# Inverting the delta rule's triangular matrix by diagonal blocks of 32 instead of in full 128 x 128 matrices

## The chip, the cores and the metric

One core of one Trainium2 chip runs the whole program. The metric is the device time of one execution in microseconds (us); the kernel before has a median of 3261.0 us over three runs (3259.91 to 3263.16).

## What is computed

One layer of a hybrid decoder for 2048 prompt tokens and 8 x 4 sample tokens: RMSNorm, one input projection (1024 to 3608 columns), a gated linear attention (GLA) group and a gated delta rule (GDN) group of four heads each, an output projection, then a gated MLP with a convolution, and a last RMSNorm. Everything is in float32. The change touches one step of the delta rule, which the reference has as a triangular solve in each chunk:

```python
kk = jnp.einsum('bhid,bhjd->bhij', ki, ki)
L = jnp.where(strict, bi[..., :, None] * kk * decay, 0.0)
eG = jnp.exp(G)[..., None]
rhs = bi[..., None] * (vi - eG * jnp.einsum('bhid,bhdv->bhiv', ki, h))
U = lax.linalg.triangular_solve(L + eye, rhs, left_side=True, lower=True, unit_diagonal=True)
```

## The kernel before, in words

The program has two halves. `mixers` runs everything up to the output projection and the second norm, `mlp` the rest. The change lies in `mixers` alone.

`mixers` walks over 16 tiles of 128 tokens (`t` from 0 to 15, `C` = 128) and then over one tile of the 32 sample tokens (`S` = 32). Each engine has its own hand-written list of instructions, in order, and they meet by semaphores. TensorE's list is the spine: its function `mixer` interleaves the mixer of tile t with large matmuls of other tiles. These come through `fill(i, j)`, which issues parts i to j-1 of 40: an even part under 16 is two steps of the output projection of tile t-1 (`project_out`, L744), any other part is two steps of the input projection of tile t+2 (`project`, L710; for the last prompt tile `project_sample`, L728, which has nothing from part 24 on). One part of `project` is 2 matmuls of 128x128 weights by 451 columns, which the profile shows as 4 MATMUL instructions: each float32 matmul is two of them.

The matrix of the delta rule is made and inverted like this, for four heads at once, each a 128 x 128 matrix with the heads side by side (512 columns):

- TensorE makes k k^T in bank 5 (L907) and q k^T in bank 7 (L911); VectorE multiplies the first by the decay (`lt`, L1671) and sets `s_lt_made`; then come the squares' sum (L1675), `ab` (L1678), `kh` (L1683), three small ones (L1688 to L1691), `vb` (L1693) and the scaled q (L1697).
- The inverse is built by doubling, level by level: `a` = 0 to 6 joins diagonal blocks of span 1, 2, 4, ... 64 (`SPANS`, `l` = 6 - `a`). GpSimd cuts out the part of `lt` that belongs to the level with a mask of 0 and 1 (`ltm`, L647, 128 x 512) and clears the other half of a product buffer (`pp`, L654).
- In level `a` TensorE computes `P` = L_a^T times the inverse `xi` (in `block_products`, L940 for the whole width and L945 for strips of 32 or 64 columns), VectorE scales it by -beta (L1754), and TensorE makes both the update of the inverse and that of its transpose `xit`, so two products into banks 3 and 4. VectorE adds them to `xi` (L1785) and `xit` (L1789). Level 0 takes transposes in place of products (L972, L1008). In level 5 only `xi` is updated; in level 6 `xi` is turned (L978), VectorE copies a part of it (L1777), and only `xit` is updated.
- `xit` and `vb` give U (L1022), U the state update (L1049) and the output (L1055, L1056). Only `xit` is read after the inverse.

Between these steps TensorE's list holds fills: part 22 after L972, 23 after `P` of level 1, then one or two parts after each product group, up to part 36 before L1022. `turn_y(0)` and `turn_y(1)` (L770) turn the normed output of tile t-1 in level 1; `turn_y(1)` waits until ScalarE has emptied the bank of projection group 3, whose last part is fill 23 (L1170). `turn_mixed(0)` (L934) stands before level 5. VectorE does other things in the same levels: `keep_gla` (L1703) in level 0, `sum_squares` (L1727) and `keep_y_half` (L1470, twice) in level 1, `subtract_known` (L1713) in level 2, `gate_out(0)` (L1735) in level 3. SyncE's list issues the DMAs in a fixed order.

The instruction of the level products, where `k` is a strip of 32 or 64 rows of the result, so that four or two strips stand in different column groups of the array:

```python
width = max(S, 2 * SPANS[l])
for b in range(0, N, width):
    k = slice(b, b + width)
    x = pe.matmul(packed(out[k, b // 2:(b + width) // 2], l), left[:, k], blocks(right[:, k], l, r),
                  start=True, stop=True)
```

## Time and profile before

| | |
|---|---|
| device time, three runs | 3259.91, 3261.0, 3263.16 us |
| span of the profiled execution, first to last instruction | 3255.5 us |
| median of the runs less this span | 5.5 us |
| TensorE busy over the span | 3173.5 us (97%) |
| VectorE, ScalarE, GpSimd busy | 2029.6, 833.7, 580.7 us |
| mean granted TensorE clock | 0.988 of full speed |
| `mixers` (until the MLP's first matmul) | 1600.66 us |

No time of its own is given for the profiled execution, so the 5.5 us around its span is taken from the runs' median. Engines: PE is TensorE's matmul, DVE VectorE, ACT ScalarE, POOL GpSimd, SPq the queue of SyncE, which issues DMAs. A row of the timeline gives start, length, engine, line, operation, tensors, shapes, and the count of instructions merged in it; lengths of merged matmuls overlap the next row's start, since matmuls are pipelined, so what a group costs is read from its start to the start of the next group. For TensorE a shape such as 128*32 128x16 is the weights' rows times their columns, then the rows and columns of what is streamed.

### The profile page before, as it was taken

To read this page: it belongs to the slowest core of one execution; us is meant where nothing else is said; L and a number is where in the kernel's file an instruction comes from. 1 tells how busy PE (TensorE), PEld (TensorE's weight loads), DVE (VectorE), ACT (ScalarE), POOL (GpSimd) and SP (SyncE) were. 2 spreads that over 40 slices of the span, in tenths; PEclk is the share of its full clock that TensorE was granted. 3 is DMA by queue.
4 is the path that set the end of the run, shared out by engine and by line. 5 is a ranking of instruction groups with operands and counts; after the bars stand their busy time and mean duration, and the time that the engine had idled before them with its cause. 6 is when DMAs were issued, how large, how long until landed. Compare 5 with 4: busy or idle time off the path is not lost.

```text
span 3255.5 us, 56610 instructions
## 1 busy us (share of the span) xinstructions
PE 3173.5 (97%) x22353; PEld 2088.1 (64%) x22353; DVE 2029.6 (62%) x4672; ACT 833.7 (26%) x1743; POOL 580.7 (18%) x935
## 2 busy tenths in 40 slices
PE   7999999999999999997799999999999999999998
PEld 4555565566655565554577777777767767777765
DVE  2556666655566665655565666666676666666668
ACT  2222333223223333233321112111232211221213
POOL 1111111111111110112331211121053121111110
PEclk9999999999999999997899999999999999999999
DMA  7022222222222222215611111111133111111112
GB/s 242 27 67 85 85 77 75 85 67 69 66 75 85 85 66 85 80 52 159 205 50 39 52 52 39 39 52 39 39 124 119 48 43 52 39 39 39 47 31 78
DMA packets 223188, 236.37 MB, mean 73 GB/s; under 512 B 14204, under 2 KB 167332, under 8 KB 222931
## 3 DMA queue, kind: packets, MB, share of 16 engines
q1 hardware_dynamic: 222931, 232.81, 22.7%
q8 instruction: 177, 2.90, 0.4%
q14 instruction: 80, 0.66, 0.1%
HBM read 203.10 MB, written 29.67 MB: 72 GB/s over the span
## 4 chain that ended last, share of the span: by engine, by line
PE 50%; DVE 1%; issue 0%; ACT 0%; DVEq 0%
PE mlp_bank L2139 33%; PE mlp_bank L2213 15%; PE mlp_bank L2227 2%; PE mlp_bank L2219 0%; DVE mcv L2588 0%; DVE arena L2552 0%; DVE acc L2649 0%; DVE arena L2553 0%; PE mlp_bank L2238 0%; ACT raw L2331 0%; PE mlp_bank L2225 0%; DVE mcv L2592 0%; DVE arena L2560 0%; DVE arena L2557 0%; DVE raw L2520 0%
## 5 line engine op out<-in xcount | busy, mean ns | idle before, releaser
L710 PE MATMUL mixer_bank<-arena,hnt 128*128 128x451 f32 x2048 | 862.5, 552 | 9.2 <-DMA arena<-in_w_in_dram 8.4
L2139 PE MATMUL mlp_bank<-arena,ws 128*128 128x256 f32 (+1 forms) x2816 | 646.2, 383 | 3.8 <-DVE raw L2526 3.8
L2139 PEld LDWEIGHTS mlp_bank<-arena,ws 128*128 128x128 f32 x2816 | 535.7, 190 | 85.8 <-DVE raw L2526 4.6
L710 PEld LDWEIGHTS mixer_bank<-arena,hnt 128*128 128x128 f32 x2048 | 365.8, 190 | 298.0 <-issue 291.5
L2213 PE MATMUL mlp_bank<-arena 128*128 128x512 f32 x1120 | 493.8, 593 | 1.0 <-DVE arena L2560 1.0
L2621 DVE TENSOR_TENSOR acc<-acc,mlp_bank 128x512 f32<-128x512 f32 x560 | 370.8, 686 | 55.5 <-PE mlp_bank L2213 54.8
L2213 PEld LDWEIGHTS mlp_bank<-arena 128*128 128x128 f32 x1120 | 213.1, 190 | 235.2 <-issue 206.2
L647 POOL TENSOR_TENSOR ex<-dtt,level 128x512 f32<-128x512 f32 (+1 forms) x114 | 142.9, 1254 | 935.6 <-DVE dtt L1671 637.3
L2588 DVE SCALAR_TENSOR_TENSOR mcv<-raw,cf,mcv 128x512 f32<-128x512 f32 (+2 forms) x352 | 262.8, 762 | 50.3 <-ACT mcv L2302 41.5
L2139 PE MATMUL mlp_bank<-arena 128*128 128x256 f32 (+1 forms) x1056 | 250.1, 387 | 5.6 <-PEq L2731 4.6
L744 PE MATMUL mixer_bank<-wo,th 128*128 128x512 f32 x512 | 248.0, 607 | 2.9 <-DMA wo<-in_w_out_dram 2.2
L2139 PE MATMUL mlp_bank<-arena,wu 128*128 128x256 f32 (+1 forms) x1056 | 246.1, 383 | 0.9 <-ACT raw L2331 0.9
L2139 PEld LDWEIGHTS mlp_bank<-arena 128*128 128x128 f32 x1056 | 202.1, 192 | 57.3 <-issue 26.6
L2139 PEld LDWEIGHTS mlp_bank<-arena,wu 128*128 128x128 f32 x1056 | 200.8, 190 | 48.9 <-issue 19.1
L1170 ACT ACTIVATE proj<-mixer_bank,x_rs 128x451 f32<-128x451 f32 x128 | 81.3, 635 | 558.3 <-PE mixer_bank L710 526.4
L2532 DVE TENSOR_TENSOR raw<-raw,mlp_bank 128x256 f32<-128x256 f32 (+1 forms) x88 | 37.5, 426 | 273.9 <-PE mlp_bank L2139 273.9
L2285 ACT COPY raw<-mlp_bank 128x256 f32<-128x256 f32 (+1 forms) x88 | 33.1, 376 | 494.4 <-PE mlp_bank L2139 494.4
L744 PEld LDWEIGHTS mixer_bank<-wo,th 128*128 128x128 f32 x512 | 93.4, 191 | 100.7 <-issue 89.8
L2526 DVE TENSOR_TENSOR raw<-raw,mlp_bank 128x256 f32<-128x256 f32 (+1 forms) x88 | 37.4, 425 | 190.1 <-ACT raw L2331 190.1
L1522 DVE SCALAR_TENSOR_TENSOR cv<-cx,cw,cv 128x128 f32<-128x128 f32 x576 | 154.7, 345 | 0.0
L2302 ACT ACTIVATE mcv<-raw,cf 128x512 f32<-128x512 f32 (+2 forms) x176 | 127.0, 721 | 103.4 <-DVE raw L2532 90.3
L1785 DVE TENSOR_TENSOR qe<-qe,mixer_bank 128x256 f32<-128x256 f32 x80 | 33.9, 424 | 127.0 <-PE mixer_bank L945 127.0
(368 smaller groups left out, 3577.9 us busy)
## 6 DMA issues: line engine op xcount, KB each, us to landing
wo<-in_w_out_dram SPq DMA_DIRECT2D x260, 256.0 KB, 2.9
arena<-in_w_up_dram SPq DMA_DIRECT2D x44, 512.0 KB, 4.9
wu<-in_w_up_dram SPq DMA_DIRECT2D x44, 512.0 KB, 4.9
arena<-in_w_down_dram SPq DMA_DIRECT2D x40, 512.0 KB, 4.0
arena<-in_w_in_dram SPq DMA_DIRECT2D x7, 1804.0 KB, 16.0
xc<-in_x_t_dram SPq DMA_DIRECT2D x16, 512.0 KB, 4.3
xt<-in_x_prompt_dram SPq DMA_DIRECT2D x16, 512.0 KB, 5.0
xr<-in_x_prompt_dram SPq DMA_DIRECT2D x16, 512.0 KB, 3.6
```

The costliest lines, as they stand in the source:

```text
L647: gp.tensor_tensor(ltm[0:N, :, 0:N], lt[0:N, :, 0:N], level[0:N, l, 0:N].unsqueeze(1).to_broadcast([N, H, N]), ALU.mult)\
L710: x = pe.matmul(bank[ring(g)][0:N, 0:GW], hnt[:, k, 0:N], w[:, k, g * GW:(g + 1) * GW], start=(k == 0), stop=(k == KT - 1))
L744: pe.matmul(bank[e if t == TILES else 0][0:N, :], mixt[k // H][:, k % H, 0:N], wo[i % 4][:, :], start=(k == 0), stop=(k == KT - 1)).then_i ...
L1170: act.activation(proj[0:N, g * GW:(g + 1) * GW], bank[ring(g)][0:N, 0:GW], ACT.Identity, scale=x_rs[0:N, :]).then_inc(s_proj_out, 1)
L1522: x = dve.scalar_tensor_tensor(out=dst, in0=src, scalar=cw[:, c, tap:tap + 1], in1=dst, op0=ALU.mult, op1=ALU.add)
L2139: x = pe.matmul(out[:, 0:N], left[:, k, :], xb[:, slot, k, g * N:(g + 1) * N], start=first and k == 0, stop=k == HK - 1, skip_group_check= ...
L2213: pe.matmul(bank[4 + o % 4][:, :], left, right, start=True, stop=True).then_inc(s_down_done, 1)
L2227: x = pe.matmul(out[0:N, :], act_[a + j][:, t * C:t * C + N], right[j][:, e * 512:e * 512 + 512], start=(j == 0 and t < 8), stop=(j == 1))
L2302: act.activation(cv[e][:, 0:n], raw[p][e][:, c0:c0 + n], ACT.Identity, scale=cf[p][:, e, 0:1])\
L2532: dve.tensor_tensor(v, v, q_bank[:, 0:N], ALU.add).then_inc(s_q2_added, 1)
L2588: x = dve.scalar_tensor_tensor(out=dst, in0=src, scalar=w, in1=dst, op0=ALU.mult, op1=ALU.add)
L2621: dve.tensor_tensor(v, v, bank[4 + o % 4][:, :], ALU.add).then_inc(s_y_added, 1)
```

## The change

For the prompt tiles the inverse is kept as the four diagonal blocks of 32 rows, one below the other in 128 partitions and 32 columns a head (`xd`, 128 x 128 for all heads), until span 16 is joined.

- VectorE makes the four diagonal blocks of `lt` first, in four instructions of 32 partitions by 128 columns (`ld`), and the other columns, 32 to 127, after the squares' sum. GpSimd cuts all five small levels out of `ld` at once (`lsm`, five instructions of 128 x 128), clears `xit`, and later makes the copy of the blocks' lower three quarters (`xa`) with a column of 0 and 1.
- Level 0: VectorE turns `lsm`'s first level (32 x 32 blocks), scales and adds the unit matrix in four instructions, and turns the result (`xdt`). TensorE has nothing to do in this level; the fill 22 that stood between its two steps stands ahead of level 1.
- Levels 1 to 4: TensorE's product has 32 rows by 32 columns of weights and 16 columns streamed, for four heads and four blocks, all into bank 5; the update is a single product of the same size into bank 3. VectorE scales (128 x 64), adds (128 x 64), and turns `xd` into `xdt` (128 x 128) itself; in level 4 it turns the four blocks into `xit`.
- Level 5 multiplies only the single 32 x 32 blocks (8 products, then 12), level 6 single 64 x 64 blocks (4, then 4), with plain copies by VectorE in place of additions.
- The masks `level` are half as wide; `small`, `unit_s` and `below` are new and set up once, the copies of the first two by seven VectorE instructions before tile 0. The sample tile keeps its two levels; one of its weight buffers moves from `level` to `cx`.

```diff
         uu = shared(ex_, 2)
+        xa = qe_[:, 0:256].rearrange("p (h i) -> p h i", h=H)
+        xd = xa[:, :, 0:S]
+        newd = qe_[:, 256:512]
+        lsm = qe_[:, 1024:1024 + NS * H * S].rearrange("p (a h i) -> p a h i", a=NS, h=H)
+        xdt, l0, ld = (ex_[:, 128 * i:128 * i + 128].rearrange("p (h i) -> p h i", h=H) for i in range(3))
...
@@ -205,8 +214,9 @@
         uu_s = ltm[:, 0, :]
         kh_s = kh[:, 0, :]
         wo_s = [proj[:, 512 * i:512 * i + 512] for i in range(7)]
-        wo_s += [v.rearrange("p a b -> p (a b)") for v in (level[:, 0:4, :], qka[:, :, :], lt[:, :, :],
+        wo_s += [v.rearrange("p a b -> p (a b)") for v in (qka[:, :, :], lt[:, :, :],
                                                            hgla[:, :, :], hgdn[:, :, :])]
+        wo_s.insert(7, cx[:, :, :].rearrange("p c i -> p (c i)")[:, 1048:1560])
...
-                inv = list(reversed(levels))
-                base = NL * t
-                for a, l in enumerate(inv):
-                    turned_later = not sample and a == NL - 2
+                if not sample:
+                    gp.wait_ge(s_rows_copied, 1)
+                    gp.wait_ge(s_ld_made, n)
+                    for a in range(NS):
+                        gp.tensor_tensor(lsm[:, a, :, :], ld[:, :, :],
+                                         small[:, NS - 1 - a, :].unsqueeze(1).to_broadcast([C, H, S]), ALU.mult)\
+                            .then_inc(s_ltm_made, 1)
+                    gp.memset(xit[:, :, :], 0.0).then_inc(s_x_sides, 1)
+                    gp.wait_ge(s_x_sides, 2 * t + 1)
+                    gp.wait_ge(s_xi_new, 6 * t + 5)
+                    gp.tensor_scalar(xa[:, :, S:2 * S], xd, below[:, :], None, ALU.mult).then_inc(s_x_sides, 1)
+                    return
...
-                        continue
+                        sample_gla_out(2 * a + 1)
+                    inv_done = 7 * t + 2
+                else:
+                    quads = [slice(S * b, S * b + S) for b in range(4)]
+                    fill(22, 23)
+                    for a in range(1, NS):
+                        l = NL - 1 - a
+                        if a == 1:
+                            pe.wait_ge(s_lt_made, n)
+                        pe.wait_ge(s_ltm_made, NS * t + a + 1)
+                        pe.wait_ge(s_xi_new, 6 * t + a)
+                        for h, r in every(range(H), quads):
+                            x = pe.matmul(packed(bank[5][r, 16 * h:16 * h + 16], l), lsm[r, a, h, :],
+                                          blocks(xd[r, h, :], l, 0), start=True, stop=True)
+                        x.then_inc(s_p_done, 1)
+                        if a == 1:
+                            turn_y(0)
+                        fill(22 + 2 * a - (a == 1), 23 + 2 * a - (a == 1))
+                        if a == 1:
+                            pe.wait_ge(s_kh_made, n)
+                        pe.wait_ge(s_p_out, 6 * t + a)
+                        pe.wait_ge(s_xit_new, 7 * t + a)
+                        for h, r in every(range(H), quads):
+                            x = pe.matmul(bank[3][r, 16 * h:16 * h + 16], xdt[r, h, :],
+                                          newd[r, 16 * h:16 * h + 16], start=True, stop=True)
+                        x.then_inc(s_dx_done, 1)
+                        if a == 1:
+                            turn_y(1)
+                            fill(24, 25)
+                        fill(23 + 2 * a, 24 + 2 * a)
+                    turn_mixed(0)
+                    pe.wait_ge(s_xi_new, 6 * t + 5)
+                    for h, (lo, hi) in every(range(H), ((quads[0], quads[1]), (quads[2], quads[3]))):
+                        x = pe.matmul(bank[5][hi, S * h:S * h + S], lt[lo, h, hi], xd[lo, h, :], start=True, stop=True)
+                    x.then_inc(s_p_done, 1)
+                    fill(32, 33)
+                    pe.wait_ge(s_p_out, 6 * t + 5)
+                    pe.wait_ge(s_vb_made, n)
+                    pe.wait_ge(s_xit_new, 7 * t + 5)
...
+                        pe.matmul(bank[3][quads[1], S * h:S * h + S], xit[quads[1], h, quads[1]],
+                                  newd[quads[1], S * h:S * h + S], start=True, stop=True)
+                        for lo, hi in ((quads[0], quads[1]), (quads[2], quads[3])):
+                            x = pe.matmul(bank[4][lo, S * h:S * h + S], newd[hi, S * h:S * h + S], xit[hi, h, hi],
+                                          start=True, stop=True)
                     x.then_inc(s_dx_done, 1)
...
+                    fill(33, 34)
+                    lo, hi = slice(0, 64), slice(64, 128)
+                    pe.wait_ge(s_xi_new, 6 * t + 6)
+                    for h in range(H):
+                        x = pe.matmul(bank[5][hi, 64 * h:64 * h + 64], lt[lo, h, hi], xa[lo, h, :], start=True, stop=True)
+                    x.then_inc(s_p_done, 1)
+                    fill(34, 35)
+                    pe.wait_ge(s_p_out, 6 * t + 6)
+                    pe.wait_ge(s_xit_new, 7 * t + 6)
+                    for h in range(H):
+                        x = pe.matmul(bank[4][lo, 64 * h:64 * h + 64], newd[hi, 64 * h:64 * h + 64], xit[hi, h, hi],
+                                      start=True, stop=True)
+                    x.then_inc(s_dx_done, 1)
+                    fill(35, 36)
+                    inv_done = 7 * n
...
                 dve.wait_ge(s_kk_done, n)
-                dve.wait_ge(s_ltm_made, NL * t)
-                dve.tensor_tensor(lt[0:N, :, 0:N], heads(5)[0:N, :, 0:N], dtt[0:N, :, 0:N], ALU.mult)\
-                    .then_inc(s_lt_made, 1)
+                dve.wait_ge(s_ltm_made, NS * t)
+                if sample:
+                    dve.tensor_tensor(lt[0:N, :, 0:N], heads(5)[0:N, :, 0:N], dtt[0:N, :, 0:N], ALU.mult)\
+                        .then_inc(s_lt_made, 1)
+                else:
+                    for b in range(4):
+                        r = slice(S * b, S * b + S)
+                        x = dve.tensor_tensor(ld[r, :, :], heads(5)[r, :, r], dtt[r, :, r], ALU.mult)
+                    x.then_inc(s_ld_made, 1)
                 dve.wait_ge(s_k_squared, n)
                 dve.wait_ge(s_k_lned, t)
                 dve.tensor_reduce(kss[0:N, :], ksq[0:N, :, :], AX_X, ALU.add).then_inc(s_k_summed, 1)
+                if not sample:
+                    dve.wait_ge(s_ld_made, n)
+                    dve.tensor_tensor(lt[:, :, S:C], heads(5)[:, :, S:C], dtt[:, :, S:C], ALU.mult).then_inc(s_lt_made, 1)
                 dve.wait_ge(s_qk_done, n)
                 dve.wait_ge(s_dti_made, n)
                 dve.tensor_tensor(ab[0:N, :, 0:N], heads(7)[0:N, :, 0:N], dti[0:N, :, 0:N], ALU.mult)\
...
+                def first_level():
+                    dve.wait_ge(s_ltm_made, NS * t + 1)
+                    dve.transpose(l0, lsm[:, 0, :, :]).then_inc(s_l0_turned, 1)
+                    dve.wait_ge(s_l0_turned, n)
+                    for h in range(H):
+                        x = dve.scalar_tensor_tensor(out=xd[:, h, :], in0=l0[:, h, :], scalar=nbeta[:, h:h + 1],
+                                                     in1=unit_s[:, :], op0=ALU.mult, op1=ALU.add)
+                    x.then_inc(s_xi_new, 1)
+                    dve.wait_ge(s_xi_new, 6 * t + 1)
+                    dve.transpose(xdt, xd).then_inc(s_xit_new, 1)
+
+                def scale_product(a, r, width):
+                    v = newd[r, 0:H * width].rearrange("p (h i) -> p h i", h=H)
+                    dve.wait_ge(s_p_done, 6 * t + a)
+                    dve.tensor_tensor(v, bank[5][r, 0:H * width].rearrange("p (h i) -> p h i", h=H),
+                                      nbeta[r, :].unsqueeze(2).to_broadcast([r.stop - r.start, H, width]), ALU.mult)\
+                        .then_inc(s_p_out, 1)
+
...
+                def later_levels():
+                    every_row = slice(0, C)
+                    quads = [slice(S * b, S * b + S) for b in range(4)]
+                    for a in range(1, NS):
+                        l = NL - 1 - a
+                        scale_product(a, every_row, S // 2)
...
+                        dve.wait_ge(s_dx_done, 6 * t + a)
+                        v = blocks(xd, l, 0)
+                        dve.tensor_tensor(v, v, packed(bank[3][:, 0:64].rearrange("p (h i) -> p h i", h=H), l), ALU.add)\
                             .then_inc(s_xi_new, 1)
-                    if a and a != NL - 2:
-                        v = blocks(xit[0:N, :, 0:N], l, 1)
-                        dve.tensor_tensor(v, v, packed(heads(4)[0:N, :, 0:N // 2], l), ALU.add)\
-                            .then_inc(s_xit_new, 1)
-                    elif a == 0:
-                        dve.tensor_tensor(xit[0:N, :, 0:N], unit, heads(4)[0:N, :, 0:N], ALU.add)\
-                            .then_inc(s_xit_new, 1)
-                        if not sample:
-                            dve.wait_ge(s_xit_new, NL * t + 1)
-                            dve.memset(heads(4)[:, :, 0:C // 2], 0.0).then_inc(s_sides_cleared, 1)
-                    if a == 1 and not sample:
-                        sum_squares()
-                        if out:
-                            if last_prompt:
-                                keep_y_half(t, C, 0)
-                            keep_y_half(t, C, 1)
-                    if a == 2 and not sample:
-                        subtract_known()
-                    if a == 3:
-                        gate_out(0)
+                        dve.wait_ge(s_xi_new, 6 * t + a + 1)
+                        if a < NS - 1:
+                            dve.transpose(xdt, xd).then_inc(s_xit_new, 1)
+                        else:
+                            dve.wait_ge(s_x_sides, 2 * t + 1)
+                            for r in quads:
+                                x = dve.transpose(xit[r, :, r], xd[r, :, :])
+                            x.then_inc(s_xit_new, 1)
+                        if a == 1:
+                            sum_squares()
+                            if out:
+                                if last_prompt:
+                                    keep_y_half(t, C, 0)
+                                keep_y_half(t, C, 1)
+                        if a == 2:
+                            subtract_known()
+                        if a == 3:
+                            gate_out(0)
+                    scale_product(NS, every_row, S)
+                    dve.wait_ge(s_dx_done, 6 * t + 5)
+                    dve.wait_ge(s_x_sides, 2 * n)
+                    dve.tensor_copy(xa[quads[1], :, 0:S], bank[3][quads[1], 0:C].rearrange("p (h i) -> p h i", h=H))\
+                        .then_inc(s_xi_new, 1)
+                    for lo, hi in ((quads[0], quads[1]), (quads[2], quads[3])):
+                        x = dve.tensor_copy(xit[lo, :, hi], bank[4][lo, 0:C].rearrange("p (h i) -> p h i", h=H))
+                    x.then_inc(s_xit_new, 1)
+                    lo, hi = slice(0, 64), slice(64, C)
+                    scale_product(6, hi, 64)
+                    dve.wait_ge(s_dx_done, 6 * n)
+                    dve.tensor_copy(xit[lo, :, hi], bank[4][lo, 0:256].rearrange("p (h i) -> p h i", h=H))\
+                        .then_inc(s_xit_new, 1)
+                if sample:
+                    sample_inverse()
+                else:
+                    first_level()
+                    keep_gla()
+                    later_levels()
```

## Rows read from the trace of the kernel before

**Rows 1.** The profile's busy time, share of the span and instructions.
```profile
PE 3173.5 (97%) x22353; PEld 2088.1 (64%) x22353; DVE 2029.6 (62%) x4672; ACT 833.7 (26%) x1743; POOL 580.7 (18%) x935
```
**Rows 2.** Busy time by stage: stretch, its length, PE, PEld, DVE, ACT, POOL, clock, DMA.
```profile
800.00:893.00 93.00, 92.61 (x967) 54.88 (x967) 58.22 (x178) 27.85 (x59) 12.31 (x15) 1.00 0.24 77
1430.00:1530.00 100.00, 78.57 (x1014) 48.65 (x1013) 57.68 (x178) 28.86 (x56) 24.78 (x33) 0.84 0.45 130
```
**Rows 3.** What TensorE waited for from 112 to 1430 us: sum, times, longest.
```profile
PE mixer_bank L945 <- DVE qe L1763: 2.4, 15, 0.2
```
**Rows 4.** TensorE's timeline through the inverse of one tile (t = 8).
```profile
845.25 0.66 PE L972 MATMUL mixer_bank<-ident,ex 128*128 128x128 f32 x4
...
848.02 0.45 PE L945 MATMUL mixer_bank<-qe,ex 128*32 128x16 f32 x32 [0.16 <-DVE qe L1763]
848.40 0.66 PE L770 MATMUL mixer_bank<-ident,xr 128*128 128x128 f32 x4
848.89 1.68 PE L710 MATMUL mixer_bank<-arena,hnt 128*128 128x451 f32 x4
850.71 0.45 PE L945 MATMUL mixer_bank<-ex,qe 128*32 128x16 f32 x32
850.99 0.46 PE L945 MATMUL mixer_bank<-qe,ex 128*32 128x16 f32 x32
...
855.37 1.78 PE L710 MATMUL mixer_bank<-arena,hnt 128*128 128x451 f32 x4
857.08 0.73 PE L945 MATMUL mixer_bank<-qe 128*32 128x16 f32 x64
...
869.23 0.66 PE L945 MATMUL mixer_bank<-qe,ex 128*64 128x32 f32 x16
...
873.74 1.00 PE L940 MATMUL mixer_bank<-qe,ex 128*128 128x64 f32 x8
874.57 0.61 PE L978 MATMUL mixer_bank<-ident,qe 128*128 128x128 f32 x4
875.01 1.68 PE L710 MATMUL mixer_bank<-arena,hnt 128*128 128x451 f32 x4
876.53 1.00 PE L940 MATMUL mixer_bank<-qe 128*128 128x64 f32 x8
...
880.45 1.05 PE L1022 MATMUL mixer_bank<-th,qe 128*128 128x128 f32 x8
```
**Rows 5.** TensorE's timeline, same tile: row-tiled products of the GLA levels.
```profile
821.13 0.99 PE L844 MATMUL mixer_bank<-qe,ex 64*32 64x16 f32 x96
822.05 1.98 PE L744 MATMUL mixer_bank<-wo,th 128*128 128x512 f32 x4
```
**Rows 6.** The other engines' timelines in the same tile.
```profile
841.48 0.69 DVE L1671 TENSOR_TENSOR dtt<-mixer_bank,dtt 128x512 f32<-128x512 f32 x1 [5.16 <-PE mixer_bank L907]
...
844.81 0.68 DVE L1697 TENSOR_TENSOR cv<-cv,egrow 128x512 f32<-128x512 f32 x1
...
847.80 1.42 DVE L1703 SCALAR_TENSOR_TENSOR hgla<-hgla,ex,mixer_bank 64x128 f32<-64x128 f32 x4
842.25 1.27 POOL L647 TENSOR_TENSOR ex<-dtt,level 128x512 f32<-128x512 f32 x1 [38.76 <-DVE dtt L1671]
850.61 0.64 ACT L1170 ACTIVATE proj<-mixer_bank,x_rs 128x451 f32<-128x451 f32 x1 [7.18 <-PE mixer_bank L710]
```
**Rows 7.** TensorE's timeline in the sample tile: products on one 32*32 tile.
```profile
1564.06 0.42 PE L940 MATMUL mixer_bank<-qe,ex 32*32 32x16 f32 x8
1564.41 0.64 PE L888 MATMUL mixer_bank<-arena 128*32 128x128 f32 x16
```
**Rows 8.** Tile 15 and after: TensorE's timeline, then SyncE's.
```profile
1501.95 0.63 PE L945 MATMUL mixer_bank<-qe,ex 128*32 128x16 f32 x32
...
1522.72 2.08 PE L1022 MATMUL mixer_bank<-th,qe 128*128 128x128 f32 x8 [0.51 <-DVE qe L1789]
1539.27 4.61 SPq L446 DMA_DIRECT2D wo<-in_w_out_dram  x4
```

207 lines of the change are left out of this document (80 added, 127 removed).

## The prediction, written before the changed kernel was run

> **What bounds the kernel now.** I read the page's busy times first: TensorE works 97% of the span and VectorE 62% [rows 1]. The stages say the same where the change lies: a tile of the prompt takes about 92 us, and in the stretch that holds it TensorE is busy 92.6 of 93.0 us at full clock, VectorE 58, GpSimd 12 [rows 2]. The list of waits leaves nothing over: from 112 to 1430 us, fourteen tiles, TensorE's only waits of note are 15 of 0.16 us, for the first update of the inverse [rows 3]. So in tiles 0 to 14 what TensorE no longer has to do is worth its own length, unless a helper comes late. Tile 15 differs: its fills end at part 24, TensorE is busy 78.6 of 100 us at a mean clock of 0.84, and a chain that goes back and forth between TensorE and VectorE sets the time [rows 2]. The MLP half is not touched. The last view is TensorE's timeline through one inverse, and the ledger comes from it.
>
> **Before, one tile.** From L972 to L1022 it is 880.45 - 845.25 = 35.20 us [rows 4]. In it lie 15 fills (parts 22 to 36) at 1.52 us (875.01 to 876.53), 22.8 us, and three sets of four transposes (`turn_y` twice, `turn_mixed`) at 0.49 (848.40 to 848.89), 1.47 us. The inverse has the rest, 10.9 us. Part of that is hidden in the fills: between two strip-tiled groups a fill takes 857.08 - 855.37 = 1.71 in place of 1.52, so 0.2 us for going out of the tiling and into it.
>
> **After, the same stretch.**
> - Level 0 leaves TensorE: eight transposes gone. Fill 22 stays and covers.
> - Levels 1 to 4: eight groups of 32 instructions with 16 columns streamed. Today's such group costs 0.38 us (848.02 to 848.40) or, without a change of tiling behind it, 0.28 (850.71 to 850.99) [rows 4]. The new one has 32 rows in place of 128. The nearest row with fewer rows, the GLA products on 64 rows, gives 0.92 us for 96, so 0.31 for 32 [rows 5]. Against that, 8 instructions that all stand on one 32 x 32 tile take 0.35, so 1.4 for 32 [rows 7]. Bounds 0.28 to 1.4; I take 0.38, since four different tiles are used in turn as today: 3.04 us. The second product of each update, into the transpose, is gone.
> - Level 5: 16 and 24 instructions. By the 0.28 group 0.14 and 0.21; by today's group of this level at most 0.66 each (its length, 869.23). I take 0.30 and 0.35, as only two or three tiles are in use.
> - Level 6: 8 instructions each of 64 x 64. From half of the 0.66 row, 0.33, to today's 0.83 for 128-column weights (873.74 to 874.57). I take 0.45 each, 0.90; the four transposes L978 go.
> - Changes of tiling: twelve tiled groups at 0.2 us are 2.4 us, of which level 6 is new. Bounds 0 and 0.4 a group.
> - Waits: 0.5 us, from the next part.
> Sum 22.8 + 1.47 + 3.04 + 0.65 + 0.90 + 2.4 + 0.5 = 31.76, so 3.44 us less a tile.
>
> **The waits that take the place of work.** VectorE starts at 841.48 and gets to the end of L1697 by 845.49 [rows 6]. At 0.60 us from start to start for 512 columns (0.15 for 128, 0.20 with its fixed part) the four `ld` pieces and the 384 columns of `lt` take 1.3 in place of 0.6, so L1697 ends at 846.2. Behind it stand `first_level`'s turn (0.3), four short scaled additions (0.4) and two hand-overs (0.1 each): `xi_new` at 847.0 to 847.1. TensorE reaches level 1 at 845.25 + 1.62 = 846.9: a wait of 0.15, like today's 0.16. The queue behind this wait is TensorE's whole list. No DVE transpose is in the trace; from a quarter of L1671's 0.69 to all of it, 0.17 to 0.69, and I take 0.3, near the low end because the elements are a quarter. The other turns run under products or fills. GpSimd's first mask needs 1.27 / 4 + 0.1, about 0.4 us, after 842.4, and all five end by 844.5 [rows 6]; nobody waits. Next `turn_y(1)`: ScalarE frees its bank 0.66 us after fill 23 ends (850.61 + 0.64 = 851.25 today) [rows 6], which today's double product covers; the single one leaves 0.35 us bare. `keep_gla` (1.42 us [rows 6]) stands ahead of the first scaling and ends at 848.9, under fill 23, which ends at 849.6. The copies of level 5 and 6 run under fills 33 to 36.
> Together 0.5 us a tile (0 to 1.5). The setup's seven VectorE copies, about 1 us, stand where VectorE waits 1.3 us for ScalarE anyway: I take 0.3 us.
>
> The Trainium skill, in "VectorE: DVE Perf Modes", section "The three transpose paths", gives 311 ns for a 128 x 128 transpose in bf16 and 32 x 32 blocks only; no run here shows it yet, and by it the term would be the same.
>
> **Tile 15.** From the product of level 2 to L1022 it takes 1522.72 - 1501.95 = 20.8 us, nearly bare [rows 8]. A level after is a shorter chain (two products of 0.5 at half clock, 64 columns scaled and added in 0.15 each): I put 13 us. Its start comes 1.8 us earlier. But SyncE issues the next output weights only from 1539.27 on, at 4.61 us for four [rows 8], in a fixed order behind 19 loads and 8 stores whose start moves by 1.8 us only. Of 9 us I let 6 through (0 to 10).
>
> **Sum.** Tiles 0 to 14 give 15 x 3.44 = 51.6, tile 15 gives 6, the setup takes 0.3: 57 us. The profiled span, 3255.5, becomes 3198.5; with the 5.5 us that lie between it and the median, 3204 us. A change of 0.2%, 6.5 us, is about what a measurement of this kernel tells from none.
>
> **Rivals.**
> - *One bank for four row groups.* Today products that stand on different rows of the array write to different banks (L844: `e` = 0 in bank 5, `e` = 1 in bank 7) [rows 5], and no row shows two row groups in one bank. The new ones write from all four to bank 5, then 3. If they then go one at a time, the price is that of rows 7, 44 ns each: 1.4 in place of 0.38 us, eight times, 8.2 us a tile, so 3204 + 15 x 8.2 = 3327 us, slower than before. The mechanism decides from (3.44 + 3.04) / 256 = 25 ns per instruction on. For it: nothing measured. Against: each quadrant of the bank is written by one row group only. 7%.
> - *VectorE late.* If a turn costs 0.7 us and more, or the short pieces cost their fixed part, level 1 starts 0.7 us later and the first update, behind the turn and `keep_gla`, about as much: 2.1 us a tile are left, 3224 us. For it: VectorE is fully queued from 841.48 to 850 in this stretch [rows 6]. 14%.
> - *No overlap by rows.* If a 32 x 32 group costs what both old products did, 0.67 us, the gain shrinks by 2.3 us a tile: 3239 us. 6%.
> - *Cheaper than that.* Groups of 0.28, no extra changes of tiling, no waits: 1.8 us more a tile, and tile 15 in full: 3204 - 27 - 3 = 3174 us; half of this is as likely as all of it. 15%.
> - *It does nothing*, because late helpers use up the 3.4 us: 3261. 3%.
>
> The Trainium skill, "TensorEngine Tiling (Array Packing)", section "Gotcha 1: PSUM Pressure", says that different row tiles cannot access the same PSUM bank at the same time. Taken to the letter it is the first rival; no row of before tries it.
>
> **Chances.** The forecast as it stands, 3190 to 3218, has 55%; the rivals 7, 14, 6, 15 and 3. The likeliest gives 3204. To hold 8 in 10 the range takes in the half of the cheaper case and the late VectorE: 3184 to 3232. Faster by more than 0.2% are forecast, late VectorE, no overlap and cheaper, 0.90; within 0.2% 0.03; slower 0.07.
>
> **What would show it.** Tile period 88.5 us against 91.9; no TensorE group in level 0; groups of 32 MATMUL 32*32 at 0.38 us from start to start; the wait for `xd` about 0.15 us and one of 0.35 us before the second L770; in tile 15 about 13 us from level 2 to L1022, then a wait for `wo`. Wrong it would be if the 32*32 groups took over 0.8 us, or if TensorE's waits in tiles 1 to 14 summed to over 15 us.

## The result and the profile after

| | before | after |
|---|---|---|
| median of four runs each, same chip, us | 3260.45 (3257.47 to 3263.16) | 3220.86 (3216.74 to 3222.4) |
| ratio, 95% interval | 1 | 0.9876 (0.9862 to 0.989) |
| span of the profiled execution, us | 3255.5 | 3220.2 |
| the same two kernels, second comparison, us | 3260.78 | 3215.87 |
| the same two kernels, third comparison, us | 3259.91 | 3216.67 |

The change makes the kernel 40 to 45 us faster, 1.2 to 1.4%. The forecast was 57 us and 3204 us in all; the measured times lie inside the range of 3184 to 3232, and one of the three medians, 3220.86, lies above the 3190 to 3218 of the forecast as it stands. The page's busy times of after, against [rows 1]:

```profile
PE 3131.1 (97%) x20241; PEld 2026.3 (63%) x20241; DVE 2010.0 (62%) x4807; ACT 832.6 (26%) x1743; POOL 467.0 (15%) x840
```

TensorE lost 42.4 us of work and 2112 instructions and is still busy 97% of a shorter span. VectorE has 135 instructions more and is 19.6 us less busy, GpSimd is 113.7 us less busy. So the bound is the same as before. The stages of after, against [rows 2] (stretch, its length, PE, PEld, DVE, ACT, POOL, clock, DMA share, GB/s):

```profile
782.00:872.00 90.00, 88.83 (x835) 50.69 (x834) 56.21 (x184) 27.34 (x57) 5.07 (x9) 1.00 0.25 78
1395.00:1497.00 102.00, 80.05 (x920) 49.12 (x920) 62.66 (x204) 32.74 (x78) 18.04 (x27) 0.84 0.44 124
```

In the middle of the prompt TensorE now stands still for 1.2 us in 90, where it was 0.4 in 93. The list of waits of after, from 112 to 1400 us (sum, times, longest), says for what, against the 2.4 us of [rows 3]:

```profile
PE mixer_bank L1006 <- DVE qe L1819: 11.4, 14, 0.8
PE mixer_bank L787 <- ACT proj L1207: 5.0, 14, 0.4
```

The first is `xd`'s product of level 1, which waits for the second command of `first_level` on VectorE; the second is `turn_y(1)`, which waits for ScalarE to clear the bank of fill 23. The prediction had 0.15 us for the one and 0.35 for the other. Both can be seen in TensorE's timeline of after through the inverse of the same tile (t = 8), the counterpart of [rows 4]:

```profile
827.13 1.78 PE L727 MATMUL mixer_bank<-arena,hnt 128*128 128x451 f32 x4
829.72 0.44 PE L1006 MATMUL mixer_bank<-qe 32*32 32x16 f32 x32 [0.81 <-DVE qe L1819]
830.09 0.66 PE L787 MATMUL mixer_bank<-ident,xr 128*128 128x128 f32 x4
...
832.20 0.44 PE L1017 MATMUL mixer_bank<-qe,ex 32*32 32x16 f32 x32
832.99 0.66 PE L787 MATMUL mixer_bank<-ident,xr 128*128 128x128 f32 x4 [0.36 <-ACT proj L1207]
...
849.53 0.44 PE L1027 MATMUL mixer_bank<-qe,dtt 32*32 32x32 f32 x16
849.90 1.78 PE L727 MATMUL mixer_bank<-arena,hnt 128*128 128x451 f32 x4
...
853.70 0.67 PE L1044 MATMUL mixer_bank<-qe,dtt 64*64 64x64 f32 x8
854.31 1.78 PE L727 MATMUL mixer_bank<-arena,hnt 128*128 128x451 f32 x4
856.02 0.68 PE L1050 MATMUL mixer_bank<-qe 64*64 64x64 f32 x8
856.62 3.29 PE L727 MATMUL mixer_bank<-arena,hnt 128*128 128x451 f32 x8
859.75 1.05 PE L1059 MATMUL mixer_bank<-th,qe 128*128 128x128 f32 x8
```

From the start of fill 22 to L1059 it is 859.75 - 827.13 = 32.62 us, forecast 31.76. A group of 32 products on 32 x 32 tiles takes 0.37 us (829.72 to 830.09), the eight products of level 6 take 0.61 (853.70 to 854.31). The tile period, from one tile's turn of its heads to the next, fell from 92.03 to 89.86 us. VectorE's timeline of after, in the stretch that decides the first wait, beside [rows 6]:

```profile
823.35 1.19 DVE L1714 TENSOR_TENSOR ex<-mixer_bank,dtt 32x128 f32<-32x128 f32 x4 [5.15 <-PE mixer_bank L924]
...
825.29 0.56 DVE L1721 TENSOR_TENSOR dtt<-mixer_bank,dtt 128x384 f32<-128x384 f32 x1
...
827.90 0.68 DVE L1743 TENSOR_TENSOR cv<-cv,egrow 128x512 f32<-128x512 f32 x1
828.50 0.30 DVE L1816 STREAM_TRANSPOSE ex<-qe 128x128 f32<-128x128 f32 x1
828.84 0.74 DVE L1819 SCALAR_TENSOR_TENSOR qe<-ex,nbeta,unit_s 128x32 f32<-128x32 f32 x4
829.61 0.31 DVE L1823 STREAM_TRANSPOSE ex<-qe 128x128 f32<-128x128 f32 x1
829.85 1.39 DVE L1749 SCALAR_TENSOR_TENSOR hgla<-hgla,ex,mixer_bank 64x128 f32<-64x128 f32 x4
```

The chain starts at 823.35, reaches `first_level` at 828.50 and hands over at 829.6: TensorE, done with fill 22 by 828.9, stands for 0.81 us. From start to start fill 22 takes 829.72 - 827.13 = 2.59 us, where fills 26 to 29 take 1.71 each, so this wait costs the tile 0.88 us.

Tile 15 next. TensorE's timeline of after from level 2 of its inverse to the sample tile, beside [rows 8]:

```profile
1468.84 0.62 PE L1006 MATMUL mixer_bank<-qe 32*32 32x16 f32 x32
1469.83 0.62 PE L1017 MATMUL mixer_bank<-qe,ex 32*32 32x16 f32 x32 [0.36 <-DVE qe L1828]
...
1481.67 2.07 PE L1059 MATMUL mixer_bank<-th,qe 128*128 128x128 f32 x8 [0.51 <-DVE qe L1873]
...
1507.73 7.55 PE L761 MATMUL mixer_bank<-wo,th 128*128 128x512 f32 x12 [4.04 <-DMA wo<-in_w_out_dram]
...
1540.34 1.93 PE L776 MATMUL mixer_bank<-wo,th 128*32 128x256 f32 x16 [1.78 <-DVE yo L1507]
```

The chain of the levels takes 1481.67 - 1468.84 = 12.83 us where it took 20.8. But what follows gives part of it back: `wo` is waited for 4.04 us, where before it was 2.17, and TensorE gets a lower clock. The stretch from the sample tile's output product (L759 before, L776 after) to the first L1067 or L1104, in before and in after:

```profile
1578.73:1590.19 11.46, 8.80 (x81) 3.34 (x81) 7.65 (x14) 2.27 (x6) 2.65 (x2) 0.80 0.22 59
1540.34:1555.28 14.94, 13.35 (x80) 4.31 (x81) 7.28 (x14) 3.33 (x8) 4.06 (x3) 0.50 0.16 44
```

Marks that both traces have, in us from the span's start:

| mark | before | after | gain |
|---|---|---|---|
| tile 15, turn of the heads (L779, L796) | 1440.73 | 1407.03 | 33.7 |
| tile 15, end of the inverse (L1022, L1059) | 1522.72 | 1481.67 | 41.05 |
| first output product of tile 15 | 1537.16 | 1496.11 | 41.05 |
| sample tile, turn of y (L770, L787) | 1567.74 | 1530.32 | 37.4 |
| first MLP product | 1600.66 | 1565.76 | 34.9 |
| end of the span | 3255.5 | 3220.2 | 35.3 |

So fifteen tiles gained 33.7 us, tile 15 up to the end of its inverse 7.4 more, and 6.2 us of these were lost in the 84 us from there to the MLP. They add up: the wait for `wo` is 1.9 us longer, the one for `yo` 2.3 shorter (1.78 after, 4.08 before, L759), and the rest, 6.6 us, lies in three stretches where the granted clock was lower: 0.68 against 0.85 between the first output product and L861 (1.8 us besides the wait), 0.76 against 0.88 from the sample tile's turn of y to L776 (1.3), and the 0.50 against 0.80 shown (3.5). The profiled execution of before was a short one: every run of after takes 1.7 us more than its span, and 3255.5 + 1.7 is still 3.3 us under the median of 3260.45. This is why 35.3 stands here and 40 to 45 between medians.

### The profile page after: what moved, and what is told of

The parts are those of the page before. It is cut to its first block, busy times and chain, and to the rows that moved or that the text cites. A ratio compares the mean times of both kernels' runs of the same rounds, so it can differ in the third digit from the quotient of the medians.

```text
span 3220.2 us, 52008 instructions
## 1 busy us (share of the span) xinstructions
PE 3131.1 (97%) x20241; PEld 2026.3 (63%) x20241; DVE 2010.0 (62%) x4807; ACT 832.6 (26%) x1743; POOL 467.0 (15%) x840
## 4 chain that ended last, share of the span: by engine, by line
PE 50%; DVE 1%; issue 0%; ACT 0%; DVEq 0%
PE mlp_bank L2216 33%; PE mlp_bank L2290 15%; PE mlp_bank L2304 2%; PE mlp_bank L2296 0%; DVE mcv L2665 0%; DVE arena L2629 0%; DVE acc L2726 0%; DVE arena L2630 0%; PE mlp_bank L2315 0%; ACT raw L2408 0%; PE mlp_bank L2302 0%; DVE mcv L2669 0%; DVE arena L2637 0%; DVE arena L2634 0%; DVE raw L2597 0%
## 5 line engine op out<-in xcount | busy, mean ns | idle before, releaser
L2362 ACT COPY raw<-mlp_bank 128x256 f32<-128x256 f32 (+1 forms) x88 | 33.1, 377 | 496.2 <-PE mlp_bank L2216 496.2
L657 POOL TENSOR_TENSOR qe<-ex,small 128x128 f32<-128x128 f32 x80 | 33.9, 459 | 628.3 <-DVE ex L1714 628.3
L2408 ACT COPY raw<-mlp_bank 128x256 f32<-128x256 f32 (+1 forms) x88 | 33.2, 377 | 275.2 <-PE mlp_bank L2216 275.2
```

## The experiments

**The same kernel again.** The kernel of after as it is, with the first group of experiments and again with the last.

> The changed kernel once more, unaltered, as the baseline of the runs beside it: 3221 us within 3 us. What the experiments are worth is counted from this run, not from the one before.

> The changed kernel once more beside the three that follow: 3216 to 3221 us, tile period 89.87 us.

Measured: 3215.87 us (3210.71 to 3217.7), ratio 0.9857 (0.9842 to 0.9872), and 3216.67 us (3214.24 to 3219.89), ratio 0.9868 (0.9853 to 0.9883). The tile period is 89.87 us in both and the waits are the same two (12.2 us in 15 times and 5.0 in 14). So the tiles repeat to 0.01 us, while whole executions of one kernel lie up to 7 us apart. Where they part can be seen in ten microseconds of tile 15, by the view of busy times. In the first profile of after:

```profile
1449.00:1459.00 10.00, 9.14 (x68) 7.11 (x66) 5.11 (x14) 3.96 (x10) 2.58 (x6) 0.83 0.01 2
```

The same view of c_after2:

```profile
1449.00:1459.00 10.00, 8.02 (x104) 5.99 (x107) 6.59 (x21) 3.94 (x10) 2.57 (x6) 1.00 0.01 2
```

With the same instructions in the same order the granted clock was 0.83 in the one and 1.00 in the other, though in both TensorE had just stood 2.69 us for ScalarE (L891), and by the second turn of y the first is 1.4 us behind (1466.94 against 1465.50). From L776 to the sample tile's last turn of y the same kernel took 19.77 us in one and 15.68 in the other. What makes the clock fall at one time or the other is not shown. Effects on tile 15 and the sample tile under some 4 us can't be read from totals here; effects on tiles 1 to 14 can be read from the period.

**Level 1 earlier on VectorE.** `first_level` moves up, behind `begcol` and ahead of the scaled q and `vb`, whose two commands nobody on TensorE waits for so soon:

```diff
 dve.tensor_tensor(begcol[0:N, :], egcol[0:N, :], nbeta[0:N, :], ALU.mult).then_inc(s_beg_made, 1)
+if not sample:
+    first_level()
 dve.wait_ge(s_v_turned, n)
...
-                    first_level()
                     keep_gla()
                     later_levels()
```

> VectorE makes level 0 right after begcol, ahead of vb and the scaled q; nothing else moves. Theory A (the 0.81 us that TensorE waits before level 1 in each tile is VectorE's list order alone): the wait goes, the first update then waits some 0.3 us for the first scaling, which still stands behind all the same VectorE work, and the second turn of y waits about 0.2 us in place of 0.36; net 0.85 us a tile, 15 tiles, 13 us: 3208 us. Rival B (the work itself is too slow, and the wait is only moved to the first update in full): 0 to 3 us, 3218 to 3221 us.

Measured: 3204.35 us (3203.96 to 3206.68), ratio 0.9829 (0.9816 to 0.9843), 11.5 us under after; period 88.98, 0.88 less. TensorE's list of waits, 112 to 1380 us:

```profile
PE mixer_bank L1017 <- issue: 3.5, 15, 0.6
```

And its timeline at the same place as above:

```profile
822.47 0.44 PE L1006 MATMUL mixer_bank<-qe 32*32 32x16 f32 x32
822.85 0.66 PE L787 MATMUL mixer_bank<-ident,xr 128*128 128x128 f32 x4
...
825.23 0.44 PE L1017 MATMUL mixer_bank<-qe,ex 32*32 32x16 f32 x32 [0.21 <-issue]
825.75 0.66 PE L787 MATMUL mixer_bank<-ident,xr 128*128 128x128 f32 x4
```

The 0.81 us are gone and arrive in the total nearly whole (15 x 0.88 = 13.2 expected from the period, 11.5 found). That the period gives 0.88 for a wait of 0.81 is the 2.59 - 1.71 from above. A second thing shows: L1017 now starts 2.38 us after L787 in place of 2.11, and the second L787 0.52 after it in place of 0.79. What one wait gained the other lost. The second L787 starts 2.40 us after fill 23 in after and 2.41 us after it here, since ScalarE clears the bank only when fill 23 is done; TensorE, with one product in between, waits that time out at the one place or at the other.

**The same, and the GLA state update behind the first scaling.** In addition:

```diff
-                    keep_gla()
                     later_levels()
...
                         scale_product(a, every_row, S // 2)
+                        if a == 1:
+                            keep_gla()
```

> As the run before, and keep_gla moved behind the first scaling. Theory A: the first update does not wait any more, but the second turn of y then waits for ScalarE, which starts when fill 23 ends; so nothing is added: 3208 us. Rival C (the first update's wait is what counts, ScalarE does not bind): another 0.3 us a tile, 3203 us.

Measured: 3205.57 us (3203.91 to 3206.92), ratio 0.983 (0.9816 to 0.9843), period 88.98, as without the second move. The waits, same view:

```profile
PE mixer_bank L787 <- ACT proj L1207: 5.0, 14, 0.4
```

L1017 waits no more, so it was `keep_gla` ahead of the first scaling that held it, and the 0.36 us for ScalarE are back in full. The order on VectorE is worth nothing as long as ScalarE's bank comes at the same time.

**The turn of y behind fill 24.** After as it is, with two calls exchanged, so that a fill covers ScalarE:

```diff
-                            turn_y(1)
                             fill(24, 25)
+                            turn_y(1)
```

> The changed kernel with the second turn of y behind fill 24 in place of ahead of it. Theory D (TensorE waits 0.36 us a tile for ScalarE to empty the bank of fill 23, and the single update no longer covers it): the wait goes in 14 tiles, 5 us: 3216 us. Rival E (VectorE's keep_y_half for this turn comes 1.5 us later and pushes the scaling of level 2 past its fills): 3221 us or more.

Measured: the period fell to 89.49, 0.38 less, and the wait for ScalarE left the list; only L1006's 12.2 us stand there. The total was 3215.25 us (3211.66 to 3218.05), ratio 0.986 (0.9845 to 0.9875), 0.6 under the same kernel without the edit. In the profiled execution tile 0 took 88.96 us in place of 87.26, at a mean clock of 0.94 in place of 0.96. The edit changes nothing in tile 0, which has no y to turn, and the run of SyncE's stores below has 88.94 there as well; so this belongs to the execution, not to the edit. The gain of the period is shown, that of the total isn't resolved.

**All three together.** First level early, state update behind the first scaling, turn behind fill 24.

> Level 0 early, keep_gla behind the first scaling, and the second turn of y behind fill 24, together. If A and D hold, neither VectorE nor ScalarE is waited for in tiles 1 to 14: tile period 88.6 us against 89.87 of the changed kernel and 88.98 of the run with level 0 early; 3200 us. If ScalarE's wait is only shifted (to fill 24's bank): 88.98 us and 3205 us.

Measured: 3206.22 us (3200.36 to 3206.93), ratio 0.9827 (0.9814 to 0.9841); period 89.12, not 88.6 and above the 88.98 of the first edit alone. The totals of the two, from different comparisons, don't differ clearly. TensorE's list of waits:

```profile
PE mixer_bank L727 <- DVE yo L1507: 6.7, 14, 0.5
```

And the place in its timeline:

```profile
826.23 0.44 PE L1017 MATMUL mixer_bank<-qe,ex 32*32 32x16 f32 x32
...
827.16 1.75 PE L727 MATMUL mixer_bank<-arena,hnt 128*128 128x451 f32 x4 [0.49 <-DVE yo L1507]
```

Fill 24 writes to the bank that held the first half of y, and `keep_y_half` takes it away. That command now stands behind `keep_gla` (1.42 us). An edit that takes one wait away put another in its place. The expectation's second case had named the place, the bank of fill 24, but ScalarE as the one waited for; the trace names VectorE.

**The removed product put back, in cost alone.** The update's product of levels 1 to 4 is issued twice into the same place:

```diff
-for h, r in every(range(H), quads):
+for again, h, r in every(range(2), range(H), quads):
     x = pe.matmul(bank[3][r, 16 * h:16 * h + 16], xdt[r, h, :],
```

> The changed kernel with the update product of levels 1 to 4 issued twice into the same place, so that a tile has four more groups of 32 instructions, about as many as the second update product had before. TensorE-bound theory: 0.28 us each, 1.1 us a tile, period 91.0 us, 17 us in all, 3233 us. If the tiles are paced by another engine by now: period 89.9 us, 3216 us. If row groups in one bank do hinder each other and the fills hide it: over 0.38 us each, period over 91.4 us.

Measured: 3233.51 us (3230.77 to 3235.12), ratio 0.9915 (0.99 to 0.9931), 17.6 us over after in another comparison; period 90.72, 0.86 more, and 15 x 0.86 = 12.9 of the 17.6 stand in the tiles. TensorE's timeline, levels 2 and 3:

```profile
843.86 0.44 PE L1006 MATMUL mixer_bank<-qe 32*32 32x16 f32 x32
...
845.94 0.73 PE L1017 MATMUL mixer_bank<-qe,ex 32*32 32x16 f32 x64
...
848.31 0.44 PE L1006 MATMUL mixer_bank<-qe 32*32 32x16 f32 x32
```

From one level to the next it is 4.45 us, where after has 836.61 to 840.77, 4.16: 0.29 for 32 instructions, 9 ns each. Three of the four sets pay it, 0.87 us in all; the one of level 1 is swallowed by the wait for ScalarE, which left the list. So in these levels work on TensorE counts at its full length, except beside a wait.

**Four transposes in front of level 1.** They turn the unit matrix into the bank that level 0 used, so TensorE does something while `first_level` runs:

```diff
 pe.wait_ge(s_lt_made, n)
+for h in range(H):
+    pe.transpose(heads(5)[:, h, :], ident[:, :], ident[:, :])
 pe.wait_ge(s_ltm_made, NS * t + a + 1)
```

> The changed kernel with four 128 x 128 transposes of the unit matrix put ahead of level 1, as level 0 had them before. If TensorE stands idle there for 0.81 us, they cost nothing: period 89.9 us, 3216 to 3220 us, and the wait before L1006 falls to about 0.35 us. If TensorE paces the tile there: 0.44 us each tile, period 90.3 us, 7 us more.

Measured: 3217.85 us (3213.83 to 3221.91), ratio 0.9871 (0.9855 to 0.9886); period 89.87, unchanged. In the list of waits the first has shrunk from 0.81 to 0.37 us each:

```profile
PE mixer_bank L1008 <- DVE qe L1821: 5.6, 15, 0.4
```

Half a microsecond of TensorE's work per tile cost nothing. With the doubled product this frames it: at the start of level 1 TensorE is idle and VectorE decides, in levels 2 to 4 TensorE decides. For levels 5 and 6 there is only the list of waits, which has none.

**Level 6 in strips of 32 columns.** Each of its two sets of products is cut in two, with 32 weight columns each:

```diff
-for h in range(H):
-    x = pe.matmul(bank[5][hi, 64 * h:64 * h + 64], lt[lo, h, hi], xa[lo, h, :], start=True, stop=True)
+for h, j in every(range(H), (quads[2], quads[3])):
+    x = pe.matmul(bank[5][j, 64 * h:64 * h + 64], lt[lo, h, j], xa[lo, h, :], start=True, stop=True)
...
-for h in range(H):
-    x = pe.matmul(bank[4][lo, 64 * h:64 * h + 64], newd[hi, 64 * h:64 * h + 64], xit[hi, h, hi],
+for h, j in every(range(H), (0, 1)):
+    x = pe.matmul(bank[4][quads[j], 64 * h:64 * h + 64],
+                  newd[hi, 64 * h + S * j:64 * h + S * j + S], xit[hi, h, hi],
```

> The changed kernel with the two products of level 6 cut into two strips of 32 weight columns each, 16 instructions on two column groups in place of 8 on one. Theory H (a 64 x 64 group takes 0.6 us, not 0.45, because loads and products on one place of the array follow one another; two places overlap): 0.40 us each, 0.4 us a tile, period 89.46 us, 6 us in all. Rival I (what counts is the 64 columns streamed through the same rows): 0.6 us each, period 89.87 us.

Measured: 3216.46 us (3213.58 to 3220.45), ratio 0.9871 (0.9856 to 0.9886), period 89.79, 0.08 less. In TensorE's timeline:

```profile
853.23 0.64 PE L1044 MATMUL mixer_bank<-qe,dtt 64*32 64x64 f32 x16
...
855.51 0.64 PE L1050 MATMUL mixer_bank<-qe 64*32 64x64 f32 x16
856.08 3.30 PE L727 MATMUL mixer_bank<-arena,hnt 128*128 128x451 f32 x8
```

Twice the instructions on half the weight columns take 0.57 us for 0.61. The 0.40 of theory H fails, and rival I, 0.6 as before, is nearly what came out; that the 64 streamed columns are the reason isn't shown by this one edit.

**SyncE's queue.** First the stores of the last projections and of both states, 13 commands, go behind the last output weights (`last_wo(8, 16)`), since those weights came late:

```diff
 sp.dma_start(cwt, ffn_taps).then_inc(s_early_w, 16)
+last_wo(4, 8)
+last_wo(8, 16)
 sp.wait_ge(s_proj_out, GROUPS * (TILES + 1))
...
-last_wo(4, 8)
...
 sp.dma_start(gdn_p, hgdn[:, :, :]).then_inc(s_states_stored, 16)
-last_wo(8, 16)
```

> The changed kernel with 13 of SyncE's stores (8 of the convolution state, 5 of the prompt states) moved behind the last loads of the output weights. Theory F (in the sample tile TensorE waits 4.0 us for an output weight because SyncE's queue has these stores ahead of it): the wait falls to 0 to 1.3 us, and the sample tile's L1104 comes some 3 us earlier against tile 15; in the total 3 us, which the spread of single runs may hide: 3213 us. Rival G (the DMA engines' bandwidth sets the landing, not the queue): the wait stays at 3 to 4 us.

Measured: 3218.0 us (3216.36 to 3220.96), ratio 0.9867 (0.9852 to 0.9883): no gain. TensorE's waits from 1380 to 1600 us:

```profile
PE mixer_bank L776 <- DVE yo L1507: 5.1, 1, 5.1
...
PE mixer_bank L761 <- DMA wo<-in_w_out_dram: 1.0, 2, 0.6
```

The wait for `wo` fell from 4.0 to 1.0 us (3.1 and 2.5 in the other two profiles of after), and that for `yo` at L776 rose from 1.8 to 5.1 (2.3 and 2.2 in the other two). `yo` can't be written before its old content is stored in `resid`, and SyncE issues that store behind all weights of the sample tile. SyncE's timeline of after shows the same order (start, length of the issues):

```profile
1503.59 1.79 SPq L456 DMA_DIRECT2D wo<-in_w_out_dram  x4
...
1523.92 3.96 SPq L553 DMA_DIRECT2D proj<-in_w_out_dram  x7
...
1531.35 0.45 SPq L467 DMA_DIRECT2D resid<-yo  x1
```

So next the `resid` store goes ahead of the twelve late weight loads too (with a semaphore of its own for the last five of them):

```diff
+sp.wait_ge(s_out_out, 2 * t)
+sp.dma_start(resid[(t - 1) * C:t * C, :], yo[:, :]).then_inc(s_resid_stored, 16)
 sp.wait_ge(s_conv_stored, 16 * (NB + 1))
 sp.wait_ge(s_va_copied, TILES + 1)
...
-    sample_wo(i, wo_s[i - 4], s_wos_loaded)
+    sample_wo(i, wo_s[i - 4], s_wos_loaded if i < 11 else s_wos_late)
```

> The 13 stores behind the output weights, as in the run e_sp, and the store of the last prompt tile's residual ahead of the sample tile's 12 late weight loads in place of behind them (the last five get a semaphore of their own). Theory J (SyncE's queue is what holds the sample tile: VectorE waits for this store to land before it turns out y, and TensorE's L776 waits for that): VectorE's wait of 3.6 us for resid goes to under 1 us, TensorE's wait before L776 from 2 to 5 us to under 1 us, and the wait for a weight stays at about 1 us; 5 us less than the changed kernel. Rival K (DMA bandwidth): the waits stay within 1 us of what they were.

Measured: 3215.99 us (3213.05 to 3216.71), ratio 0.9862 (0.9847 to 0.9877). Both waits have gone or shrunk: from the sample tile's first turn of y to its output product it is 6.84 us in place of 10.02, and `wo` costs 1.1. But the next turn behind that product now waits:

```profile
1540.90 0.63 PE L957 MATMUL mixer_bank<-ident,th 32*128 32x32 f32 x4 [3.21 <-DVE th L1787]
```

In after this wait was 0.64 us, in c_after2 0.58. From the sample tile's first turn of y to the MLP it is 31.8 us (1528.92 to 1560.75), in c_after2 31.1 and in after, at its lower clock, 35.4: most of what the product no longer waits for is waited for one step later. Also tile 15 was 3.0 us later by its second turn of y (1468.50 against 1465.50 in c_after2), before either edit can act (the first moved command is issued at 1501.46). The same ten microseconds as above:

```profile
1449.00:1459.00 10.00, 9.69 (x60) 8.51 (x60) 3.76 (x11) 4.33 (x10) 2.37 (x6) 0.70 0.01 2
```

The clock fell earlier still. Each of the two waits shrinks when its command moves ahead in the queue, so the queue's order makes them; that mending it shortens the kernel isn't shown.

**A version that beats both.** `first_level` early, `keep_gla` behind the first half of y (so that fill 24's bank is free in time), the turn behind fill 24, level 6 in strips, and SyncE's order of the last experiment. The order on VectorE is the part that is new:

```diff
                         scale_product(a, every_row, S // 2)
                         if a == 1 and out and not last_prompt:
                             keep_y_half(t, C, 0)
+                        if a == 1:
+                            keep_gla()
```

> All that helped or should: level 0 early, keep_gla behind keep_y_half(0), the second turn of y behind fill 24, level 6 in strips, and SyncE's order. Period 89.87 - 0.88 - 0.38 - 0.4 = 88.2 us, so 25 us in 15 tiles, and 5 us in the sample tile: 3188 us against 3218 of the changed kernel. If waits are only passed on as they were with keep_gla ahead of keep_y_half(0): period 88.7 us or more, 3196 us.

Measured: **3195.78 us** (3194.79 to 3195.91), ratio to before 0.9803 (0.9789 to 0.9816): 64 us under before, 21 under after of the same comparison. The period is 88.53, and from 112 to 1380 us TensorE's list of waits is empty. 15 x (89.87 - 88.53) = 20.1 us explain nearly all of it, and the 1.34 us a tile are the 0.88, 0.38 and 0.08 of the single edits. The expected 88.2 had 0.4 for the strips, and the 5 us expected from SyncE's order don't show in the total. The total is the 3196 us of the expectation's second case, but not for its reason: no wait is passed on here. TensorE's timeline at level 1:

```profile
820.56 0.44 PE L1012 MATMUL mixer_bank<-qe 32*32 32x16 f32 x32
820.93 0.66 PE L793 MATMUL mixer_bank<-ident,xr 128*128 128x128 f32 x4
...
823.04 0.44 PE L1023 MATMUL mixer_bank<-qe,ex 32*32 32x16 f32 x32
...
825.02 0.60 PE L793 MATMUL mixer_bank<-ident,xr 128*128 128x128 f32 x4
```

No bracket stands behind any of these lines: from the first L793 to L1023 it is 2.11 us, as in after, and the second L793 has a fill ahead of it.

## Why the prediction was right or wrong

**The bound: right.** What leaves TensorE in tiles 0 to 14 is worth its length. The doubled product shows it from one side for levels 2 to 4, the four added transposes from the other: free only where TensorE waits.

**The 32 x 32 groups: right.** 0.38 us forecast, 0.37 measured in the seven groups of levels 1 to 4 that have no wait behind them, with four row groups of the array writing to one bank. The rival *one bank for four row groups* needed 1.4 us and falls; so does *no overlap by rows*, 0.67. The page "TensorEngine Tiling (Array Packing)" of the Trainium skill, section "Gotcha 1: PSUM Pressure", says that different row tiles cannot access the same PSUM bank at the same time; here each row tile writes to partitions of its own in the bank, and 9 ns per added instruction leave no room for one at a time (44 ns in [rows 7]). The measurement decides, for tiles that each write to their own quarter; two row groups on the same partitions of a bank were not tried.

**The transpose on VectorE: right.** 0.30 us taken, 0.30 and 0.31 measured (L1816, L1823). The Trainium skill's 311 ns in "VectorE: DVE Perf Modes", section "The three transpose paths", agrees, here for float32. GpSimd's masks cost 0.42 us each, as forecast, and nobody waits for them.

**The wait ahead of level 1: wrong, 0.81 us in place of 0.15.** This is the term of the sum that was furthest off: "the four `ld` pieces and the 384 columns of `lt` take 1.3 in place of 0.6, so L1697 ends at 846.2", and behind it "four short scaled additions (0.4)". A `ld` piece of 32 partitions by 128 columns takes 0.30 us, not 0.20 (L1714, 1.19 for four), so the chain to the end of the scaled q (L1743, L1697 before) is 828.50 - 823.35 = 5.15 us long, forecast 4.72. The four additions take 0.74, not 0.4. From the chain's start to L1006 it is 6.37 us, forecast 5.57, so 0.80 too little; the wait grew by 0.66 only, as TensorE arrives 1.78 us after the start of the fill (827.13 to 828.91) and not 1.62. The short pieces do cost their fixed part: this half of the rival *VectorE late* is what happened. Its other half, an equal delay of the first update, did not: L1017 starts at 832.20 with no wait. Moving `first_level` alone brought 0.88 us of the period back. With this wait the prediction's own sign of being wrong came true: more than 15 us of TensorE's waits in tiles 1 to 14 was to show it wrong, and they are 11.4 + 5.0 = 16.4, in all three profiles of after. What that sign convicts is the term on the waits, put at 0.5 us a tile, and not the bound.

**The wait for ScalarE: right**, 0.36 for 0.35, with its cause, since the turn exchanged with fill 24 removed it.

**Level 6: wrong, 0.61 us in place of 0.45, twice.** The forecast stood between its bounds of 0.33 and 0.83, nearer the low one; 0.31 us a tile. Level 5 had 0.30 and 0.35 and took 0.37 and 0.37, another 0.1.

**The tile that was measured: 0.40 us.** [Rows 4] are of tile 8, 35.20 us from L972 to L1022. Its neighbour takes 34.80 (753.22 to 788.02), and the periods say the same: 92.03 as a rule (the prediction has 91.9), 92.44 for tile 8. The excess sits in two of its double groups, 0.79 and 0.94 us from start to start where the neighbour has 0.67 and 0.66; why they are longer isn't shown. A gain worked out against one tile carried that tile's excess fifteen times.

The three together: 34.80 - 32.62 = 2.18 us gained a tile, and the periods give 92.03 - 89.86 = 2.17. Of the 3.44 forecast, 0.40 was the tile, 0.66 the wait, 0.31 level 6, 0.09 level 5; these are 1.46 for a shortfall of 1.26, so 0.2 of other terms came out better. That is mostly the fills: without the wait the fifteen take 24.9 us, where 22.8 and 2.4 for the changes of tiling were put. Fifteen tiles and the setup gave 33.7 us in place of 51.3 (tile 0 alone gained 3.0, and the setup cost nothing: tile 0 starts at 61.46, before at 61.67).

**Tile 15: right in its chain, open in what it gives.** 13 us were put for level 2 to the end, 12.83 measured. The start of level 2, forecast 1.8 us earlier in the tile, comes 0.6 later in after (61.81 us into the tile, before 61.22) and 0.9 earlier in c_after2 (60.28). Of the "9 us I let 6 through": up to the end of the inverse tile 15 gives 7.4 us in after, 9.0 in c_after and 8.9 in c_after2; up to the MLP 1.2, 4.4 and 6.5. So one and the same kernel gives both a fifth of the forecast 6 and a little more than 6, and that the sum of tile 15 came out in c_after2 can't be counted for the forecast. What was named, SyncE's queue, takes a part: the issue of `wo` moved from 1539.27 to 1503.59, 35.7 us, while its user moved by 41.05, and the wait grew by 1.9. The larger part was not named: the granted clock on the way, 6.6 us in the profile of after. The `resid` store in the same queue makes TensorE wait too, but it did so before, and longer, so it takes nothing of the gain.

**The total.** 15 x 1.26 = 18.9 us too much in the tiles, less 0.8 that tile 0 gained beyond the others, is 18; 57 - 18 = 39, and 39.6 to 44.9 were measured. So the mechanism was right and the gain of a tile, 3.44 us forecast and 2.17 measured, was mis-sized; that the total still lies in the range is owed to the width that was given for a late VectorE. The rival *VectorE late* had 3224 us and 2.1 us a tile, which is nearer to the outcome than the forecast's own case, though only half for its reason.

## What to carry to other kernels

When a big instruction is cut into pieces for a faster engine's sake, cost each piece from a row of the same number of columns, whatever its partitions, and follow the chain that the pieces stand in up to the first instruction that the bounding engine waits for. Take a ledger's baseline from the usual tile (the period over many), not from the one that happened to be opened. And once the waits of the bounding engine are few, look who stands behind each command that is moved: three edits together had a longer tile period than one of them alone (89.12 against 88.98), until the bank of the next fill was freed in time.

## What the runs showed of the hardware that was not expected

- Four row groups of the array write to four partition quarters of one bank at the price that four column strips had before (0.38 and 0.28 us in [rows 4]): 32 instructions of 32*32 with 16 columns in 0.37 us, 32 more for 0.29, 9 ns each.
- 64*64 products with 64 columns take 76 ns each (0.61 / 8), and cutting them into column strips of 32 gives 36 ns each (0.57 / 16): the instruction count doubles and the time stays.
- VectorE pays the same for 32 partitions as for 128: 0.30 us a piece for the products of 32x128 read from a bank (L1714) and 0.29 for one of 128x128 (L1828 in level 5); 0.31 us a piece for the transposes of 32x128 in level 5 (L1850, 1.25 for four) and 0.30 for one of 128x128; a 128x32 scaled addition still costs 0.18.
- One kernel's executions differ by when the granted clock falls in tile 15: 0.83 in after and 1.00 in c_after and c_after2 over the same ten microseconds, with no difference in the instructions. A third value, 0.70, is from the kernel with SyncE's order changed, before that order can act.
